# MLP up projections in seven half-size products instead of eight, and the norm's root squared on the down projection's output

## The reference

```python
def rms_norm(x, g):
    y = xf * lax.rsqrt(jnp.mean(xf * xf, axis=-1, keepdims=True) + EPS)
    return (y * g.astype(jnp.float32)).astype(x.dtype)
...
        h = rms_norm(x, g_mlp[l])
        f = jnp.square(jax.nn.relu(jnp.einsum("bsd,df->bsf", h, w_1[l])))
        x = x + jnp.einsum("bsf,fd->bsd", f, w_2[l])
```

## Time and profile before

| | us |
|---|---|
| runs, median of 3 (2234.74 to 2234.99) | 2234.75 |
| profiled execution, span from first to last instruction | 2233.0 |
| TensorE busy in it | 2216.4 |
| VectorE busy | 1236.5 |
| ScalarE busy | 867.2 |
| GpSimd busy | 865.8 |

### The profile page before, as it was taken

How to read it: one execution, slowest core, us unless ns; L and a number is a source line. 1 busy time by engine, 2 the same in 40 slices (tenths; PEclk the granted TensorE clock), 3 DMA queues, 4 the chain that set the end, 5 groups by cost and what they waited for, 6 DMA issues and landing times.

```text
span 2233.0 us, 28460 instructions
## 1 busy us (share of the span) xinstructions
PE 2216.4 (99%) x10130; PEld 1793.9 (80%) x10130; DVE 1236.5 (55%) x1844; ACT 867.2 (39%) x1101; POOL 865.8 (39%) x188
## 2 busy tenths in 40 slices
PE   8999999999999999999999999999999999999998
PEld 6888887787888887888887888888788887888887
DVE  6999998666242246877866232236666514232233
ACT  5253464533122224666544222224566523222233
POOL 3444454543443433423224444444412244444442
PEclk9999999999999999999999999999999999999999
DMA  5233332423222223222123322322312232322322
GB/s 196 94 109 103 104 121 84 141 94 105 94 94 94 94 94 95 57 76 75 40 74 98 102 86 93 101 84 79 100 52 61 71 94 81 102 86 92 111 85 76
DMA packets 230809, 206.05 MB, mean 92 GB/s; under 512 B 13904, under 2 KB 220368, under 8 KB 230480
## 3 DMA queue, kind: packets, MB, share of 16 engines
q1 hardware_dynamic: 227328, 199.36, 28.7%
q10 hardware_dynamic: 3408, 5.70, 0.7%
HBM read 194.02 MB, written 4.19 MB: 89 GB/s over the span
## 4 chain that ended last, share of the span: by engine, by line
issue 56%; PE 28%; POOL 15%; POOLq 0%; DVE 0%; ACT 0%; ACTq 0%; DVEq 0%
POOL w_lo L577 15%; PE ps L1768 6%; PE ps L1769 6%; PE ps L1770 6%; PE ps L2295 2%; PE ps L2256 2%; PE ps L1801 1%; PE ps L1803 1%; PE ps L1802 1%; PE ps L2284 1%; PE ps L2392 1%; PE ps L2391 1%; PE ps L2390 1%; PE ps L2263 0%; PE ps L2262 0%
## 5 line engine op out<-in xcount | busy, mean ns | idle before, releaser
L577 POOL TENSOR_TENSOR w_lo<-raw,w_hi 128x2048 fp32r<-128x2048 f32 x184 | 865.6, 4704 | 1345.7 <-ACT w_hi L591 1335.1
L591 ACT ACTIVATE w_hi<-raw 128x2048 fp32r<-128x2048 f32 x183 | 349.9, 1912 | 671.3 <-PE ps L1770 420.6
L1768 PE MATMUL ps<-XH,w_hi 128*128 128x512 f32 x1136 | 450.1, 396 | 0.0
L1770 PE MATMUL ps<-XH,w_lo 128*128 128x512 f32 x1136 | 448.7, 395 | 0.0
L1769 PE MATMUL ps<-XL,w_hi 128*128 128x512 f32 x1136 | 448.7, 395 | 0.0
L1768 PEld LDWEIGHTS ps<-XH,w_hi 128*128 128x128 f32 x1136 | 212.9, 187 | 52.7 <-issue 0.7
L1769 PEld LDWEIGHTS ps<-XL,w_hi 128*128 128x128 f32 x1136 | 212.9, 187 | 52.6 <-issue 0.7
L1770 PEld LDWEIGHTS ps<-XH,w_lo 128*128 128x128 f32 x1136 | 212.9, 187 | 52.1
L1382 DVE TENSOR_TENSOR X<-X,ps 128x512 f32 x72 | 49.5, 688 | 339.8 <-PE ps L1770 176.8
L1368 DVE SCALAR_TENSOR_TENSOR tmp<-ps,rst 128x512 f32<-128x512 f32 x96 | 66.3, 691 | 257.3 <-PE ps L1770 240.2
L772 ACT ACTIVATE FH<-tmp 128x512 f32 (+1 forms) x96 | 60.8, 633 | 371.7 <-DVE tmp L1368 371.7
(11 more groups left out here) (376 smaller groups left out, 3661.2 us busy)
## 6 DMA issues: line engine op xcount, KB each, us to landing
raw<-in_w SPq DMA_DIRECT2D x64, 512.0 KB, 4.3
raw<-in_mlp_w_up SPq DMA_DIRECT2D x64, 512.0 KB, 4.4
raw<-in_mlp_w_down SPq DMA_DIRECT2D x64, 512.0 KB, 4.1
raw<-in_w_in SPq DMA_DIRECT2D x56, 512.0 KB, 4.6
raw<-in_mla_w_o SPq DMA_DIRECT2D x16, 512.0 KB, 4.8
raw<-in_w_b_out SPq DMA_DIRECT2D x16, 384.0 KB, 3.8
raw<-in_w_a_out SPq DMA_DIRECT2D x8, 512.0 KB, 4.7
raw<-in_w_o SPq DMA_DIRECT2D x8, 512.0 KB, 3.9
```

Source lines behind the costliest of these rows:

```text
L577: pool.tensor_tensor(w_lo[:, s], raw[:, s], w_hi[:, s].bitcast(F32), ALU.subtract)\
L591: act.activation(w_hi[:, s], raw[:, s], ACT.Copy).then_inc(hi_done, 1)
L1768: pe.matmul(dst, his[k], xh[k], start=start and k == 0, stop=False)
L1770: mm = pe.matmul(dst, los[k], xh[k], start=False, stop=stop and k == n - 1)
```

## The change

35 of the 44 up chunks that fall under the new loop (in each MLP from the fourth chunk on; mlp2's last quarter stays as it was) are made by a scheme of seven products: the 1024 x 256 weights are seen as 2 x 2 blocks of 512 x 128 and the activations as 2 x 2 blocks of 512 features x 256 tokens. With four sums of activation blocks (once for each MLP; SUM2, then high and low parts in BLOCKS, from gained copies XG of x) and three differences of weight blocks for each chunk (made in PSUM banks 4 to 7, then high parts WTH and low parts WTL, one of them in the place of the fourth block of w_hi and w_lo), seven products of 512 x 128 by 512 x 256 give the 128 x 256 quarters of the two output tiles after additions. `part` is one of these products, 4 k-tiles x 3 matmuls of 256 columns. Three intermediate results are copied to SN by ScalarE (`keep_part`), and VectorE adds them to what is in PSUM (`y_and_f`). Each chunk of two tiles is then handled at once: relu and square in one operation, high part by ScalarE, low part by GpSimd, or by VectorE for the last of four.

The root is no longer applied to the up products: since relu(root x a) squared is root^2 x relu(a)^2 for a positive root, the down projection's output is multiplied by the root squared (`down_scaled`) before it is added to X. The MLPs' loops are written out instead of being run as loops on the engines. The DMAs of the next stage's constants, issued by ScalarE ahead of mlp0 (2) and mlp1 (4), are issued at their ends.

```diff
+def seven(n, v):
+    if n == "mlp2" and v >= 24:
+        return False
+    return v % 8 < 4 and v >= 3
...
+            def split_lo_three(n, v):
+                s, c = v % 2, FIRST[n] + v
+                pool.wait_ge(hi_done, c + 1)
+                pool.tensor_tensor(w_lo[:, s, 1024:2048], raw[:, s, 1024:2048], w_hi[:, s, 1024:2048].bitcast(F32),
+                                   ALU.subtract)
+                pool.wait_ge(*ff("t_made", 3 * SEVEN[n, v] + 3))
+                one = [t[:, s].rearrange("p (k n) -> p k n", k=8)[:, 0:4, 0:P] for t in (w_lo, raw, w_hi)]
+                pool.tensor_tensor(one[0], one[1], one[2].bitcast(F32), ALU.subtract).then_inc(lo_done, 1)
+            def f_low(n, v):
+                u = UP[n, v]
+                pool.wait_ge(*ff("u_fh", u + 1))
+                pool.tensor_tensor(FL[:, 2 * (u % 4):2 * (u % 4) + 2], f_of(u), FH[:, 2 * (u % 4):2 * (u % 4) + 2].bitcast(F32),
+                                   ALU.subtract).then_inc(ff_sem("u_fl"), 1)
+            def mlp_pool(n):
+                last = 24 if n == "mlp2" else 32
+                for v in range(32):
+                    if (n, v) in SEVEN:
+                        split_lo_three(n, v)
+                    else:
+                        split_lo(FIRST[n] + v, v % 2)
+                    if v >= 2 and v - 2 < last and (v - 2) % 8 < 3:
+                        f_low(n, v - 2)
...
+                for k in range(KD):
+                    act.activation(XG[k // 4][:, k % 4], X[:, k], ACT.Copy, scale=col(gain, off + k))\
+                        .then_inc(ff_sem("x_gained"), 1)
...
+            def split_hi_three(n, v):
+                s, c = v % 2, FIRST[n] + v
+                act.wait_ge(raw_in[s], 16 * (c - s) + 32)
+                act.wait_ge(halves, 2 * c + 2)
+                act.activation(w_hi[:, s, 1024:2048], raw[:, s, 1024:2048], ACT.Copy)
+                act.activation(w_hi[:, s].rearrange("p (k n) -> p k n", k=8)[:, 0:4, 0:P], raw8(s)[:, 0:4, 0:P], ACT.Copy)\
+                    .then_inc(hi_done, 1)
+            def t_high(n, v, which):
+                s = v % 2
+                act.wait_ge(*ff("t_made", 3 * SEVEN[n, v] + 3))
+                if which == 0:
+                    act.activation(WTH[:, s, 0:2], ps[:, 4:6], ACT.Copy).then_inc(ff_sem("t_hi"), 1)
+                elif which == 1:
+                    act.activation(corner(w_hi, s), as_tiles(ps[:, 6]), ACT.Copy).then_inc(ff_sem("t_hi"), 1)
+                else:
+                    act.activation(WTH[:, s, 2], ps[:, 7], ACT.Copy).then_inc(ff_sem("t_hi"), 1)
+            def keep_part(n, v, which):
+                w, bank = SEVEN[n, v], 2 * (v % 2)
+                act.wait_ge(*ff("part_done", 3 * w + which + 1))
+                if which == 0:
+                    act.wait_ge(*ff("u_y", 2 * UP[n, v]))
+                    act.activation(SN[:, 2], ps[:, bank, 0:HALF], ACT.Copy).then_inc(ff_sem("part_kept"), 1)
+                elif which == 1:
+                    act.activation(SN[:, 0:2].rearrange("p a t -> p (a t)"), ps[:, bank + 1], ACT.Copy)\
+                        .then_inc(ff_sem("part_kept"), 1)
+                else:
+                    act.activation(SN[:, 3], ps[:, bank, 0:HALF], ACT.Copy).then_inc(ff_sem("part_kept"), 1)
...
+                for v in range(1, 25 if n == "mlp2" else 29):
+                    if (n, v + 1) in SEVEN:
+                        split_hi_three(n, v + 1)
+                        t_high(n, v + 1, 0)
+                    elif v > 1:
+                        split_hi(c + v + 1, (v + 1) % 2)
+                    if v == 1:
+                        sums_hi(n, range(2))
+                    if v == 2:
+                        sums_hi(n, range(2, 4))
+                    if (n, v) in SEVEN:
+                        keep_part(n, v, 0)
+                    if (n, v + 1) in SEVEN:
+                        t_high(n, v + 1, 1)
+                        t_high(n, v + 1, 2)
+                    if (n, v) in SEVEN:
+                        keep_part(n, v, 1)
+                        keep_part(n, v, 2)
+                    if (v - 1) % 8 < 4 and (n != "mlp2" or v - 1 < 24):
+                        f_high(n, v - 1)
...
+            def sums(n, j)
...
+                first, second, op = ((a21, a22, ALU.add), (SUM2[:, 0], a11, ALU.subtract), (a11, a21, ALU.subtract),
+                                     (a12, SUM2[:, 1], ALU.subtract))[j]
+                dve.tensor_tensor(SUM2[:, j % 2], first, second, op).then_inc(ff_sem("sums_made"), 1)
...
+            def t_make(n, v, which):
...
+                    dve.tensor_tensor(ps[:, 4:6].rearrange("p j (k n) -> p j k n", n=P),
+                                      r[:, :, P:2 * P].rearrange("p (j k) n -> p j k n", j=2),
+                                      r[:, 0:4].rearrange("p k (j n) -> p j k n", j=2), ALU.subtract)\
+                        .then_inc(ff_sem("t_made"), 1)
...
+                    dve.tensor_tensor(as_tiles(ps[:, 6]), r[:, 4:8, P:2 * P], as_tiles(ps[:, 4]), ALU.subtract)\
+                        .then_inc(ff_sem("t_made"), 1)
...
+                    dve.tensor_tensor(as_tiles(ps[:, 7]), r[:, 4:8, 0:P], as_tiles(ps[:, 6]), ALU.subtract)\
+                        .then_inc(ff_sem("t_made"), 1)
...
+            def y_and_f(n, v):
+                u, bank = UP[n, v], 2 * (v % 2)
+                dve.wait_ge(halves, half_at(FIRST[n] + v, 1))
+                dve.wait_ge(*ff("u_f", u))
+                if (n, v) in SEVEN:
+                    dve.wait_ge(*ff("part_kept", 3 * SEVEN[n, v] + 3))
+                    a_ = ps[:, bank:bank + 1, 0:HALF].to_broadcast([P, 2, HALF])
+                    dve.tensor_tensor(tmp[:, 0:2, 0:HALF], ps[:, bank:bank + 2, HALF:T], SN[:, 2:4], ALU.add)\
+                        .then_inc(ff_sem("u_y"), 1)
+                    dve.tensor_tensor(tmp[:, 0:2, HALF:T], a_, SN[:, 0:2], ALU.add).then_inc(ff_sem("u_y"), 1)
+                else:
+                    dve.tensor_scalar(tmp[:, 0:2], ps[:, bank:bank + 2], 0.0, None, ALU.max).then_inc(ff_sem("u_y"), 2)
+                dve.wait_ge(*ff("u_y", 2 * u + 2))
+                dve.wait_ge(*ff("u_fl", u))
+                dve.scalar_tensor_tensor(f_of(u), tmp[:, 0:2], 0.0, tmp[:, 0:2], ALU.max, ALU.mult)\
+                    .then_inc(ff_sem("u_f"), 1)
+            def f_low(n, v):
+                u = UP[n, v]
+                dve.wait_ge(*ff("u_fh", u + 1))
+                dve.tensor_tensor(FL[:, 6:8], f_of(u), FH[:, 6:8].bitcast(F32), ALU.subtract).then_inc(ff_sem("u_fl"), 1)
...
+            def down_scaled(dst, root):
+                dve.tensor_tensor(dst, dst, root, ALU.mult).then_inc(ff_sem("d_scaled"), 1)
+                scaled[0] += 1
+                dve.wait_ge(*ff("d_scaled", scaled[0]))
...
+                root = rst[:, 0:1] if n == "mlp2" else rst[:, 1:2]
+                def finish(v):
+                    if v % 8 < 4:
+                        y_and_f(n, v)
+                        return
+                    j, tiles = 2 * (v % 2), slice(2 * (v % 8 - 4), 2 * (v % 8 - 4) + 2)
+                    dve.wait_ge(halves, half_at(c + v, 1))
+                    if v == 4:
+                        dve.wait_ge(*at("n_" + n, "inv", 1))
+                        dve.tensor_tensor(root, rst[:, 1:2], rst[:, 1:2], ALU.mult).then_inc(ff_sem("root_2"), 1)
+                        dve.wait_ge(*ff("root_2", MLPS.index(n) + 1))
+                    down_scaled(ps[:, j:j + 2], root.to_broadcast([P, 2, T]))
+                    dve.tensor_tensor(X[:, tiles], X[:, tiles], ps[:, j:j + 2], ALU.add).then_inc(sig(n, "dn"), 2)
+                for j in range(2):
+                    sums(n, j)
+                for v in range(1, 25 if n == "mlp2" else 29):
+                    finish(v - 1)
+                    if v == 1:
+                        sums_low(n, 0)
+                        sums_low(n, 1)
+                        sums(n, 2)
+                        sums(n, 3)
+                    if v % 8 == 4:
+                        f_low(n, v - 1)
+                    if (n, v + 1) in SEVEN:
+                        for which in range(3):
+                            t_low(n, v + 1, which)
+                    if (n, v + 2) in SEVEN:
+                        for which in range(3):
+                            t_make(n, v + 2, which)
+                    if v == 2:
+                        sums_low(n, 2)
+                        sums_low(n, 3)
...
                 for k in range(KD):
                     dve.wait_ge(halves, half_at(c + 28 + k // 2, k % 2))
+                    down_scaled(ps[:, k % 4], rst[:, 1])
                     dve.tensor_tensor(X[:, k], X[:, k], ps[:, k % 4], ALU.add).then_inc(sig(n, "dn"), 1)
                     if k:
                         after(k - 1)
...
-                dve.wait_ge(*at(n, "inv", 1))
...
+            def seven_products(n, v, xh, xl):
...
```

(90 more changed lines are left out.)

215 lines of the change are left out of this document (124 added, 91 removed).

## The result

The changed kernel takes 2201.8 us (median of 4 runs, 2200.9 to 2203.5) where the kernel before, timed beside it, takes 2234.9 us (2234.7 to 2235.4). The ratio is 0.985, with a 95% interval of 0.984 to 0.986: 33 us faster. I had forecast 2193.0 with a range of 2175 to 2221. The time is inside that range and 0.8 us outside the forecast's own range, 2185 to 2201.

What follows compares the result with a forecast made beforehand. TensorE, busy all along, was taken as the bound: matmul count times spacing. 2233.0 - 45.1 (spacing) + 2.5 (waits) + 1 (seams) = 2191.4 profiled, 2193 in the runs (1.75 kept); own range 2185 to 2201, widened to 2175 to 2221.

Steps and rivals of the forecast that it cites:

- The spacing: Up chunks in seven products: 256-column matmuls 0.118 us apart, 9.91 us a chunk instead of 11.20, 45.1 us off over 35.
- a start stamped early: Attention stage's pair of 256-column products: the 0.17 us step after the first was not taken as real spacing, unlike 0.12.
- rival C: Seven-product chunks: weight load not hidden at 256 columns, spacing 0.145 us, +35 us, 2270; chance 0.07.
- rival A: Seven-product chunks: 256-column spacing at the weight load's pace, 0.1115 us, 64 us off, 2171; chance 0.10.
- The waits within a chunk: TensorE's wait points inside seven-product chunks: 0.01 us x 7 waits x 35 chunks = 2.5 us added (0 to 5).
- The edits priced at nothing: Written-out loops, larger instruction queue, tail, inverse root's wait and moved constants: no cost or gain; tail at worst 0.9 us twice.
- The seams: MLP starts and passages from up to down chunks: helpers in time, 3 us to spare; 0.3 us per MLP, 1 us.
- rival B: Seams: VectorE's square or t_make late behind GpSimd, first down chunk waits 2 us, 11 times: +22 us, 2215; chance 0.18.

Runs made afterwards that it cites:

- run 7: The kernel of run 5 with 32 free bytes behind the vectors, moving all placed later (x, f, sums, WTH, WTL) but not w_hi, w_lo: 2164.29 us, ratio 0.968.
- 8: The kernel of run 5 with the first three parts of each seven-product chunk 288 columns wide instead of 256, MLP values not the reference's: 2209.2 us in one run.
- run 2: The changed kernel with no chunk made in seven products, all else of the change kept: 2235.75 us, ratio 1.0003 to the kernel before.
- Run 4: The changed kernel with GpSimd waiting, before chunk 5's low weight parts in each MLP, until VectorE has squared tile pair 3: 2193.0 us, ratio 0.981.
- run 5: The kernel of Run 4, with chunk 3's first kept part waiting for the sums' low parts instead of y of tile pair 2: 2190.05 us, ratio 0.980.
- run 3: The changed kernel with WTH, WTL, SN and SUM2 placed 32 bytes further on, nothing else: 2203.1 us, ratio 0.986.
- runs 1: The changed kernel with seven products only from the ninth chunk of each MLP on, instead of the fourth: 2194.7 us, ratio 0.982.
- the two runs of 9: The kernel of run 5 with 64 or 96 free bytes behind the vectors: 2194.8 us (ratio 0.982) and 2186.5 us (ratio 0.978).
- 11: The kernel of run 7 with WTH, WTL, SN and SUM2 another 32 bytes further on: 2168.9 us, ratio 0.971.

## Why the prediction was right, and where it fell short

**The spacing** was the step on which everything hung: 0.118 us expected, 0.1181 measured over a chunk, 44.8 us off against 45.1. That it fits so closely is in part luck: the attention stage's tiles lie elsewhere, and with the tiles moved by a few dozen bytes matmuls of 256 columns were 0.113 to 0.120 us apart in the runs; the working had no term for that, and none for 0.2333 falling to 0.2299. Reading the pair in the earlier trace rows as a start stamped early held up; rival C (0.145) and rival A (0.1115) are out in this placement. Runs 7 and 8 together show that the loads, two under way at a time, don't set the 0.117.

**The waits within a chunk**, 2.5 us, cost nothing: chunks are 9.92 us with them and there is no step at a part's end. The term was 2.5 us too high, at the lower of its own bounds (0 to 5). The edits priced at nothing (loops, tail, the inverse root, constants, the instruction queue) measured nothing together in run 2.

**The seams** are the failed step: "I put 0.3 us per MLP: 1 us." They cost 9.9 us by the starts, and a stretch at the lower clock 1.7 more. The mechanism stood in the same paragraph ("with the square behind GpSimd's 4.6 us it would be 1.5 to 2 us late") and in rival B, which had it at all 11 seams; it came at 3, though L1542 was locked out in nearly every chunk. What I missed is where it comes: I followed the first quarter to t_low(3) only and checked it against chunk 3's first use of WTL, which was indeed in time. The low parts of the sums (L1530) have both inputs in SBUF like the square, and met f_low; that lateness went on to y(2) and SN, to a square of chunk 2 locked out for another 3.1 us, and by its low part to the square at the seam. I had put them under chunks 0 to 2 by their plain 1.22 us. Run 4 (one wait on GpSimd) took back 8.8 us and run 5 another 2.95; with both the kernel is at 2190.05, where the sum without the seams gives 2233.0 - 45.1 + 2.5 + 1.75 = 2192.15 for the runs, and 2189.65 without the waits too.

So the net error of 8.8 us is -2.5 for the waits that cost nothing and about +10.6 for the seams and the clock, plus less than 1 us that I can't place. The time lies inside the range because that was drawn out to 2221 for rival B, whose mechanism is the one that came; that it is only 8.8 us off owes something to two errors of opposite sign.

**What stays open.** When a wait is followed by the lower clock: 1 of 3 waits was in the changed kernel's profiled execution, 3 of 3 in run 3's, and none behind the opening stage in runs 1, 4 and 5, which have no such wait (starts 0.43 us apart from about 10 to 12.5 us, behind the waits at the very start, are in every execution, that of before too). And what in the placement sets the spacing: neither the stationary operand alone (run 7), nor the start modulo 64 bytes (the two runs of 9), nor a part's own operands (runs 7 and 11) explains it, and the same instruction on the same places has two paces within one execution. No run separated the buffers one by one, or the matmuls' operands from what the other engines use, which moved with them.

## What to carry to other kernels

When TensorE is busy all along, an exchange of instructions is priced by spacing times count, and the spacing of the new size can be had from a few neighbouring starts in another stage, to within the 3% or so that the tiles' places are worth. Then go through the first turn of the loop apart, with every piece of once-only work in it: list each VectorE instruction whose inputs are all in SBUF against GpSimd's instructions, and give GpSimd a wait where one meets a deadline. And before judging a change by one or two per cent, try both kernels with a few dozen free bytes ahead of the matmul's operands, since this alone was worth 1.2 to 1.3% here (25.8 of 2190, 29.9 of 2234.6 us). Read the spacing in more than one stretch, since one execution can hold two.

## What the runs showed of the hardware

- The place of the buffers in SBUF changes the spacing of matmuls: 512 columns from a mean of 0.2333 to 0.2299 us by 32 free bytes, 256 columns with w_hi from 0.117 to 0.113, and the whole kernel from 2190.1 to 2164.3 us; 64 bytes made it worse (2194.8 us).
- In one execution the same matmul on the same places ran at two paces: parts with w_hi took 1.36 us in 30 chunks and 1.41 in five (run 7), 512 columns on (XH, w_hi) 0.2286 us a step in one stretch and 0.2333 in another.
- A VectorE instruction with both inputs in SBUF, started 0.15 us behind GpSimd's, lasted 5.57 us instead of 1.23. GpSimd's pays too: w_lo of 557.11, begun while the second of L1530 was running, took 5.56 us, where its median was 4.62.
- A stretch of 3.4 us at a granted clock of 0.50 followed some waits of TensorE of 1.75 to 2.5 us and not others, at the same place of the same program.
